# An RWKV-7 recurrence whose transposed inverse blocks are kept on the other half of the partitions

## The reference, cut to what matters

```python
def rwkv7_scan(r, w, k, v, kk, a):
    def step(state, inp):
        r_t, w_t, k_t, v_t, kk_t, a_t = inp
        sa = jnp.einsum('bhvk,bhk->bhv', state, -kk_t)
        state = (state * w_t[:, :, None, :] + sa[..., None] * (kk_t * a_t)[:, :, None, :]
                 + v_t[..., None] * k_t[:, :, None, :])
        return state, jnp.einsum('bhvk,bhk->bhv', state, r_t)
    ...
    _, out = lax.scan(step, jnp.zeros((nB, H, N, N), F32), xs)

# rwkv7_mixer: for each of two directions (the second with time reversed)
        o = rwkv7_scan(*ins)
        bonus = jnp.sum(rh * kd * r_k.astype(F32), axis=-1, keepdims=True) * vh
        dir_out.append((group_norm(o, gn_w, gn_b) + bonus.reshape(nB, S, D)) * g.astype(F32))
```

## Time and profile before

| | before |
|---|---|
| median of 3 runs | 2591.73 us (2591.47 to 2594.94) |
| span of the profiled execution | 2590.2 us |
| TensorE busy in it | 2488.4 us, 96% |
| VectorE busy | 1104.5 us, 43% |
| ScalarE busy | 475.8 us, 18% |
| mean granted clock of TensorE | 0.992 of full speed |

### The profile page before, as it was taken

How to read it: one execution, slowest core, us unless ns; L and a number is a source line. 1 busy time by engine, 2 the same in 40 slices (tenths; PEclk the granted TensorE clock), 3 DMA queues, 4 the chain that set the end, 5 groups by cost and what they waited for, 6 DMA issues and landing times. The chain is left out here.

```text
span 2590.2 us, 80261 instructions
## 1 busy us (share of the span) xinstructions
PE 2488.4 (96%) x36137; PEld 2147.1 (83%) x36137; DVE 1104.5 (43%) x2659; ACT 475.8 (18%) x1059; POOL 179.1 (7%) x225
## 2 busy tenths in 40 slices
PE   8999999999999999999999999899999999999998
PEld 7898878789889989999989898677768677877775
DVE  4672554468211010110110102457672578775676
ACT  2112000211123223210000001410010444542000
POOL 0100000010022322210000000000000001110000
PEclk9999999999989999999999999999999999999999
DMA  7444444554589999999999998335653000020443
GB/s 228 156 147 149 162 162 149 162 163 147 208 317 407 407 407 408 407 408 407 407 407 408 407 407 277 122 98 194 220 172 130 3 7 7 7 70 25 163 172 120
DMA packets 289906, 571.50 MB, mean 221 GB/s; under 512 B 17422, under 2 KB 180244, under 8 KB 289764
## 3 DMA queue, kind: packets, MB, share of 16 engines
q1 hardware_dynamic: 289764, 569.49, 60.0%
HBM read 568.37 MB, written 5.28 MB: 221 GB/s over the span
## 5 line engine op out<-in xcount | busy, mean ns | idle before, releaser
L2669 PE MATMUL ps<-xg,ring 128*64 128x80 f32 x14336 | 508.4, 233 | 6.4 <-issue 4.8
L2669 PEld LDWEIGHTS ps<-xg,ring 128*64 128x64 f32 x14336 | 501.8, 137 | 11.0 <-issue 6.6
L2792 DVE TENSOR_TENSOR hidden<-acted,ps 128x320 f32<-128x320 f32 x64 | 28.6, 446 | 662.2 <-PE ps L2669 662.2
L2685 PE MATMUL ps<-hidden,expert_down 128*64 128x80 f32 x7168 | 258.4, 234 | 11.0 <-DMA expert_down<-in_moe_w_down_dram 5.2
L2685 PEld LDWEIGHTS ps<-hidden,expert_down 128*64 128x64 f32 x7168 | 252.8, 138 | 13.9 <-issue 9.7
L2734 ACT ACTIVATE ring<-second 128x1792 f32<-128x1792 f32 x60 | 101.9, 1699 | 212.7 <-PE ps L2669 156.3
L631 PE MATMUL ps<-xT,ring 128*128 128x256 f32 (+1 forms) x592 | 134.4, 387 | 3.0 <-PEq L474 3.0
L631 PEld LDWEIGHTS ps<-xT,ring 128*128 128x128 f32 (+1 forms) x592 | 108.0, 185 | 26.7 <-issue 3.5
L2726 POOL COPY ring<-second 128x1792 f32<-128x1792 f32 x60 | 101.0, 1683 | 311.1 <-PE ps L2669 183.8
L631 PE MATMUL ps<-ring,xT 128*128 128x256 f32 (+1 forms) x544 | 108.9, 361 | 2.2 <-PEq L1136 2.2
L631 PEld LDWEIGHTS ps<-ring,xT 128*128 128x128 f32 x544 | 96.0, 190 | 14.5 <-issue 3.0
(11 more groups left out here) (617 smaller groups left out, 3980.4 us busy)
## 6 DMA issues: line engine op xcount, KB each, us to landing
expert_down<-in_moe_w_down_dram SPq DMA_DIRECT2D x96, 1024.0 KB, 17.1
ring<-in_mlp_w_dram SPq DMA_DIRECT2D x64, 1024.0 KB, 5.3
ring<-in_moe_w_gate_dram SPq DMA_DIRECT2D x68, 896.0 KB, 16.0
ring<-in_moe_w_up_dram SPq DMA_DIRECT2D x68, 896.0 KB, 16.6
second<-in_moe_w_gate_dram SPq DMA_DIRECT2D x30, 1792.0 KB, 18.8
second<-in_moe_w_up_dram SPq DMA_DIRECT2D x30, 1792.0 KB, 19.0
ring<-in_w_xkv_dram SPq DMA_DIRECT2D x16, 1024.0 KB, 5.4
expert_down<-in_moe_w_down_dram SPq DMA_DIRECT2D x32, 512.0 KB, 16.5
```

The costliest lines, as they stand in the source:

```text
L2669: mm = pe.matmul(bank[b][o:o + HEAD, at, :], w[:, c, f * P + o:f * P + o + HEAD], xg[:, p * E_STEP + c, :], start=(p == 0 and c == 0 and a ...
L2685: mm = pe.matmul(yT[c // 4][o:o + HEAD, c % 4, :], w[:, j, c * P + o:c * P + o + HEAD], hidden[:, f, :], start=False, stop=False, skip_gro ...
L2792: dve.tensor_tensor(hidden[:, part, :], acted[:, part, :], src, ALU.mult).then_inc(hidden_ready, 1)
```

## The change

1. `XX` and `M1` become flat, by regions of four 64-column blocks. Kind 0 (the inverse) is region 0 for direction 0 and region 1 for direction 1; kind 1 (the transpose) is the other region. Kind 1 is kept on the **other** half of the partitions. `m1` writes it there by taking the other half of the columns.
2. `halves` writes its result to the other half (off-diagonal quarters), so that `Pb` lies beside kind 1.
3. `steps` reads both operands from the other half. Kind 0 goes across to its own half (off-diagonal quarters), kind 1 stays (diagonal quarters). Kind 0 and kind 1 go to different banks: region 0 is the second half of bank A(d), region 1 the first half of bank B(d).
4. `right_sides`, `solve_first`, `carry` and `solve_second` exchange halves to suit. `solve_first` of both directions writes to bank B(1) in place of G(d).
5. On PE, at each level both `halves` (with `rows` at k = 1) come first, then for each direction the filler and `steps`. The order is H0, H1, filler, S0, filler, S1.
6. The masked copies of level 0 and of `steps` take the two regions as one contiguous run; at k = 5 one region alone.
7. In the last pair `carry(i, 1)` comes before `turn(6)`.

```diff
+        def region(kind, d):
+            return kind if d == 0 else 1 - kind
+        def XX(i, d, kind, n):
+            at = (4 * region(kind, d) + n) * HEAD
+            return XXs[d][i % 2][:, at:at + HEAD]
+        FIRST = B(1)
+        def both_kinds(d):
+            return ps[:, A(d):B(d) + 1, :].rearrange("p a b -> p (a b)")[:, 4 * HEAD:]
+        def made(d, kind, n):
+            at = n * HEAD
+            if region(kind, d):
+                return ps[:, B(d), at:at + HEAD]
+            return ps[:, A(d), 4 * HEAD + at:4 * HEAD + at + HEAD]
...
                 def halves(i, k, d):
                     wait(pe, "x_ready", i, 2 * (k - 1) + d + 1)
                     for n in range(4):
                         for b in range(2):
-                            h = half(b)
-                            mm = pe.matmul(ps[h, A(d), n * HEAD:(n + 1) * HEAD], GM[d][h, n, 0, h], XX(i, d)[h, n, 0, :], start=True, stop=True)
+                            h, other = half(b), half(1 - b)
+                            mm = pe.matmul(ps[other, A(d), n * HEAD:(n + 1) * HEAD], GM[d][h, n, 0, h], XX(i, d, 0, n)[h], start=True, stop=True)
                     mm.then_inc(q["half_done"].sem, 1)
...
                     for n in range(4):
                         for kind in range(1 if k == LEVELS - 1 else 0, 2):
                             for b in range(2):
-                                h = half(b)
-                                xt, p = XX(i, d)[h, n, 1, :], Pb[d][h, n, :]
-                                at = (2 * n + kind) * HEAD
-                                mm = pe.matmul(ps[h, B(d), at:at + HEAD], p if kind else xt, xt if kind else p, start=True, stop=True)
+                                other = half(1 - b)
+                                xt, p = XX(i, d, 1, n)[other], Pb[d][other, n, :]
+                                on = other if kind else half(b)
+                                mm = pe.matmul(made(d, kind, n)[on], p if kind else xt, xt if kind else p, start=True, stop=True)
...
                 def solve_first(i, s, d):
-                    f = half(d)
+                    f, g = half(d), half(1 - d)
                     for hh in range(2):
                         at = SOLVED + hh * HEAD
-                        mm = pe.matmul(ps[f, G(d), at:at + HEAD], XX(i, d)[f, 2 * chunk(s, d) + hh, 1, :], rhs[d][f, s, hh, :], start=True, stop=True)
+                        mm = pe.matmul(ps[f, FIRST, at:at + HEAD], XX(i, d, 1, 2 * chunk(s, d) + hh)[g], rhs[d][g, s, hh, :], start=True, stop=True)
...
                             halves(i, k, d)
                             if k == 1:
                                 rows(i, d)
+                        for d in range(2):
+                            if k == 1:
                                 rest(i, 0, d)
                             elif k == 2:
                                 rest(i, 1, d)
...
                 def step(i, k, d):
-                    x = XX(i, d)[:].rearrange("p n k e -> p n (k e)")
-                    made = ps[:, B(d), :].rearrange("p (n e) -> p n e", n=4)
-                    a, e = (HEAD if k == LEVELS - 1 else 0), 2 * HEAD
-                    places = level[:, k, d * HEAD + a:d * HEAD + e].unsqueeze(1).to_broadcast([P, 4, e - a])
-                    dve.copy_predicated(x[:, :, a:e], places, made[:, :, a:e]).then_inc(q["x_ready"].sem, 1)
+                    places = level[:, k, 0:2 * HEAD].rearrange("p (r e) -> p r e", r=2).unsqueeze(2).to_broadcast([P, 2, 4, HEAD])
+                    x, fresh = (z.rearrange("p (r n e) -> p r n e", r=2, n=4) for z in (whole(i, d), both_kinds(d)[:, 0:8 * HEAD]))
+                    if k == LEVELS - 1:
+                        x, fresh, places = (z[:, region(1, d)] for z in (x, fresh, places))
+                    dve.copy_predicated(x, places, fresh).then_inc(q["x_ready"].sem, 1)
```

More of the change, by code:

```diff
@@ L3333, in chunks @@
         GM = [tmp(ctx, "GM", [P, 4, 4, P]) for _ in range(2)]
-        M1 = [tmp(ctx, "M1", [P, 4, 2, HEAD]) for _ in range(2)]
-        XXs = [[tmp(ctx, "XX", [P, 4, 2, HEAD]) for _ in range(2)] for _ in range(2)]
+        M1 = [tmp(ctx, "M1", [P, 8 * HEAD]) for _ in range(2)]
+        XXs = [[tmp(ctx, "XX", [P, 8 * HEAD]) for _ in range(2)] for _ in range(2)]
         Pb = [tmp(ctx, "Pb", [P, 4, HEAD]) for _ in range(2)]
@@ L3351, in ends, with whole @@
             return keys[d][i % 2][:, WIDTH:]
-        def XX(i, d):
-            return XXs[d][i % 2]
+        def region(kind, d):
[3 more added lines that the diff above has]
+            return XXs[d][i % 2][:, at:at + HEAD]
+        def whole(i, d):
+            return XXs[d][i % 2][:, 0:8 * HEAD]
         def gb(i, d):
@@ L3449, in begin @@
                     for d in range(2):
-                        act.activation(XX(j, d)[:].rearrange("p n k e -> p (n k) e"), eyes[:].unsqueeze(1).to_broadcast([P, 8, HEAD]), ACT.Copy).then_inc(q["x_begun"].sem, 1)
+                        act.activation(whole(j, d).rearrange("p (n e) -> p n e", e=HEAD), eyes[:].unsqueeze(1).to_broadcast([P, 8, HEAD]), ACT.Copy).then_inc(q["x_begun"].sem, 1)
                 def exps_first(j, d):
@@ L3467, in take_m1 @@
                     wait(act, "m1_done", j, d + 1)
-                    act.activation(M1[d][:].rearrange("p (t h) k e -> p h t (k e)", h=2), ps[:, A(d):B(d) + 1, 0:4 * HEAD].rearrange("p h (t x) -> p h t x", t=TT),
+                    act.activation(M1[d][:, 0:8 * HEAD].rearrange("p (x h e) -> p h x e", h=2, e=HEAD), ps[:, A(d):B(d) + 1, 0:4 * HEAD].rearrange("p h (x e) -> p h x e", e=HEAD),
                                    ACT.Copy).then_inc(q["m1_ready"].sem, 1)
@@ L3493, in take_right @@
                     wait(act, "right_done", i, 2 * s + d + 1)
-                    f = half(d)
+                    f = half(1 - d)
                     act.activation(rhs[d][f, s].rearrange("p a b -> p (a b)"), ps[f, G(d), RIGHT:RIGHT + P], ACT.Copy).then_inc(q["right_ready"].sem, 1)
@@ L3499, in take_first @@
                     f = half(d)
-                    act.activation(sa[d][f, chunk(s, d)].rearrange("p a b -> p (a b)"), ps[f, G(d), SOLVED:SOLVED + P], ACT.Copy).then_inc(q["first_ready"].sem, 1)
+                    act.activation(sa[d][f, chunk(s, d)].rearrange("p a b -> p (a b)"), ps[f, FIRST, SOLVED:SOLVED + P], ACT.Copy).then_inc(q["first_ready"].sem, 1)
                 def take_carried(i, s, d):
                     wait(act, "carried_done", i, 2 * s + d + 1)
-                    f = half(1 - d)
+                    f = half(d)
                     act.activation(rhs[d][f, s].rearrange("p a b -> p (a b)"), ps[f, G(d), RIGHT:RIGHT + P], ACT.Copy).then_inc(q["carried_ready"].sem, 1)
@@ L3581, in m1 @@
                         for kind in range(2):
-                            for hh, b in CORNERS:
+                            at = (2 * region(kind, d) + t) * HEAD
+                            for hh, on in CORNERS:
+                                b = 1 - on if kind else on
                                 a, e = KR(j, d)[half(hh), t, 0, half(b)], Bs[d][half(hh), t, half(b)]
-                                at = (2 * t + kind) * HEAD
-                                mm = pe.matmul(ps[half(b), A(d) + hh, at:at + HEAD], e if kind else a, a if kind else e, start=True, stop=True)
+                                mm = pe.matmul(ps[half(on), A(d) + hh, at:at + HEAD], e if kind else a, a if kind else e, start=True, stop=True)
                     mm.then_inc(q["m1_done"].sem, 1)
@@ L3642, in right_sides @@
                         left = GM[d][:, 2 * t + hh, 2, :]
-                        pe.matmul(ps[f, G(d), at:at + HEAD], left[:, f], values(i, t, hh), start=(hh == 0), stop=(s == 0 and hh == 1))
-                        mm = pe.matmul(ps[g, G(d), at:at + HEAD], left[:, g], values(i, t, hh), start=(hh == 0), stop=False)
+                        pe.matmul(ps[g, G(d), at:at + HEAD], left[:, f], values(i, t, hh), start=(hh == 0), stop=(s == 0 and hh == 1))
+                        mm = pe.matmul(ps[f, G(d), at:at + HEAD], left[:, g], values(i, t, hh), start=(hh == 0), stop=False)
                     if s:
                         s0 = S0[d][:].rearrange("p a b -> p (a b)")
-                        pe.matmul(ps[f, G(d), RIGHT:RIGHT + P], KR(i, d)[:, t, 0, f], s0, start=False, stop=True)
-                        mm = pe.matmul(ps[g, G(d), RIGHT:RIGHT + P], KR(i, d)[:, t, 0, g], s0, start=False, stop=False)
+                        pe.matmul(ps[g, G(d), RIGHT:RIGHT + P], KR(i, d)[:, t, 0, f], s0, start=False, stop=True)
+                        mm = pe.matmul(ps[f, G(d), RIGHT:RIGHT + P], KR(i, d)[:, t, 0, g], s0, start=False, stop=False)
                     mm.then_inc(q["right_done"].sem, 1)
@@ L3686, in carry @@
                         at = RIGHT + hh * HEAD
-                        mm = pe.matmul(ps[g, G(d), at:at + HEAD], GM[d][f, 2 * t + hh, 0, g], sa[d][f, t, hh, :], start=False, stop=(hh == 1))
```

(14 more changed lines are left out.)

## The result

| | before | changed |
|---|---|---|
| median | 2592.36 us | 2646.67 us |
| ratio to before | | 1.022 (95% interval 1.020 to 1.023) |
| span of the profiled execution | 2590.2 us | 2644.9 us |
| mean granted clock of TensorE | 0.992 | 0.969 |

Of four executions of the changed kernel one took 10789.31 us at a mean granted clock of 0.217, and the median is over the other three (2645.08 to 2654.05).

A forecast was written before the change was run, and what follows sets the result against it. TensorE and DVE were both taken as nearly full in the recurrence. 18.6 (middle pairs) + 2.1 (pair 0) - 1.5 (pair 7) took the span from 2590.2 to 2609.4, the median 1.5 above: 2611, range 2589 to 2622.

The forecast's parts named there:

- The order: At each level H1 waits for copy 1, filler and S0 queue behind it; a middle pair gets 3.1 us longer.
- the walk: Step times through a pair's levels, counted from H0 of k = 1; a middle pair's last copy at 26.38.
- the sum: 18.6 for six middle pairs, 2.1 for pair 0, -1.5 for pair 7: 19.2 us on the profiled span.
- The quarters: S on four quarters costs 0.63 before a filler, some 0.12 less before its own shape; its copy starts 0.44 earlier.
- Rival 1: Quarters don't run in parallel; copy 0 comes 0.44 later at k = 2, 3, 4: 10.5 us, 2621; chance 0.10.
- rival 4: TensorE's gaps of up to 1.9 us lower its granted clock, every block doubles: beyond 2625; chance 0.03.
- Rival 2: The reorder pays: S's wait for ACT goes, DVE runs nearly without idle time, 15 us in all, 2577; chance 0.13.
- The other edits: Masked copies, `take_m1`, eye copy, `m1`, `solve_first`: taken as 0; copies at most 5 us either way; `carry` 0 to -0.6.

The follow-up runs named there:

- the clock held: The changed kernel plus three unused 128x256 products between H0 and H1 at k = 2, 3 and 5: 2610.9 us, ratio 1.008.
- only k = 5 filled: The changed kernel plus three unused 128x256 products between H0 and H1 at k = 5 alone: 2614.7 us, ratio 1.010.

## Why the prediction was right and wrong

**The order, right.** TensorE does not pass a waiting H1: the filler and S0 start only behind it, in every level. (Once H1 runs, the first records of S0 can start ahead of its last two, at 2209.86 against 2209.90 at k = 4 of pair 3 of the changed kernel.) With the clock held, the copies stand within 0.3 us of the walk, the pair takes 38.3 (38.5 forecast), and the kernel 2610.9 against 2611. The terms agree less well than their sum. With the clock held a middle pair is 2.9 us longer (3.1 forecast). Pair 0 has its last copy at 25.99 after H0 (walk 25.35), so 2.8 longer and not 2.1. Pair 7 has it at 25.46 (walk 22.4): it kept the time it had before, and the -1.5 of the sum was not there. That kernel is 21 us over the kernel before timed beside it, where the sum had 19. So 2611 was met in part by luck, the errors of pair 7 and of the middle pairs having opposite signs.

**The quarters, right.** S1 of k = 3 in the changed kernel, at full clock, and the H behind it (the first row is the first two records of S alone):

```profile
2207.44 0.27 PE L3689 MATMUL ps<-Pb,XX 64*64 64x64 f32 x2
...
2207.96 0.63 PE L3676 MATMUL ps<-XX,GM 64*64 64x64 f32 x16
```

S takes 0.52, where the earlier trace rows had 0.98 and the prediction 0.51. Rival 1 is out. At k = 5 S has only 16 records, all on the two diagonal quarters, and with the clock held it takes 0.61 before its filler; that the walk's 0.63, read from 32 records on four quarters, came so near is luck.

The trace bears out neither limit that the prediction cited, for this shape. The Trainium skill, "TensorE: Matmul & The Clock Gate", section "Wait — 56ns, not 53.3ns?", has matmuls start no closer than about 25 ns; here 32 records start in 0.52, 16 ns each. The Trainium skill, "TensorEngine Tiling (Array Packing)", section "Gotcha 1: PSUM Pressure", has different row tiles not use one PSUM bank at the same time; here two row halves write to one bank, on different partitions, in those same 0.52.

**The clock, wrong.** The step that failed is the clock's term. It stood at nothing in the sum and as rival 4, with a chance of 0.03, on the ground that the granted clock was 1.00 where the gaps were 0.48. The walk itself gave gaps of up to 1.9 us, and at full clock the traces show 1.5 to 1.6 in three levels of a middle pair (k = 2, 3 and 5). The rows chosen had no gap of that size, so they could not price it, and the missing price was taken for a small chance. The trace before reached further than those rows, and it speaks for both sides:

```profile
1908.33 1.98 PE L539 MATMUL ps<-cols,ident 128*128 128x512 f32 x4 [1.57 <-DVE u L2217]
```
```profile
1904.00:1912.00 8.00, 6.43 (x16) 2.71 (x15) 7.61 (x14) 2.90 (x8) 2.19 (x2) 1.00 0.92 292
2048.00:2055.00 7.00, 6.29 (x8) 2.71 (x9) 3.45 (x12) 4.16 (x8) 0.00 (x0) 0.51 0.08 20
```

A single gap of 1.57 us left the clock at 1.00. But just ahead of the first levels it fell to 0.51 for 7 us, with no gap over 1.1 us in the 20 us before. So in the kernel before, too, a fall did not need a long gap, and a chance of 0.03 was too small. The measured price is 36 us: 2646.7 less 2610.9. Of the 9.0 us that a pair like pair 3 lost, 2.9 are the order and 6.1 the clock. The low stretch also ran on into the solves, behind the levels, where the prediction had looked only for time that might be given back. Rival 4's outcome, beyond 2625, is what came. Its "every block would double" is a little too much: at half clock H takes 1.05 to the next block (2196.88 to 2197.93) in place of 0.62. And since DVE and ACT kept their pace, 21 us at half clock cost 6.1.

**The other side, wrong in its ground and right in its size.** Rival 2 had the reorder pay and DVE run without idle time, 2577. That time was measured (2574) with the order taken **out**: the quarters alone bring it, because a copy then comes before DVE is through with its own work. The prediction took the 0.44 us of the quarters into the walk but never asked what they give without the order.

**The other edits.** The new form of the copies lasts as long as the old one (about 0.72, and 0.77 for the two of k = 5), as taken. No run parts bank B(1), the exchanged halves and `m1` from the quarters; together they cost nothing that would hide the gain.

## What to carry to other kernels

On TensorE here a product that waited held up everything behind it in the list. So before moving one forward, follow what it waits for, and compare the chain that then starts behind that wait with the work that the other engine has of its own in that time. Here the chain was longer, and the difference was lost. When a change leaves TensorE with new idle spells that the old trace does not show, hold a run with the gaps filled against it: here the lower clock cost 6.1 us a pair and the waits 2.9. A faster product is worth what the next engine can take up, and a reorder meant to help it has to be timed apart from it.

## What the hardware showed

- Four quarters of TensorE's array work at once. 32 records of 64x64 need 0.52 us in place of 0.98 at full clock, though two row halves write to one bank, on different partitions.
- The granted clock fell to 0.50, that is 1.2 GHz, after idle spells of 0.3 to 0.5 and 1.6 us with one H between them, in a kernel whose TensorE is 95% busy as a whole. The same spells at k = 2, with only k = 5 filled, left it at 1.00 in five of six middle pairs.
- Half clock on this stretch costs less than double, since DVE and ACT keep their pace (a copy of 512 columns lasts 0.72 to 0.73 at either level): 21 us of a pair at half clock cost 6.1.
